# Output products moved among mixer C's last tasks, and four weight units split on GpSimd

## The chip, the cores and the metric

The kernel runs on one core of a Trainium2 chip. The metric is the device time of one execution in microseconds, as the median of several runs. The core has a matrix engine (TensorE), a vector engine (VectorE, DVE in the rows), an activation engine (ScalarE, ACT), a general engine (GpSimd, POOL) and a queue that issues transfers (SyncE, SP). They run side by side and meet only at semaphores. TensorE writes to PSUM, eight banks of 128x512 f32; the rest lies in SBUF.

## The reference

Two layers over 512 tokens of width 1024. Each is one input projection that feeds three token mixers, an output projection, a layer norm, a squared-ReLU MLP and another layer norm:

```
proj = x @ w_in[l]                        # 2578 columns, split into q, k, v, ... of the three mixers
o_a = diff_attention(...)                 # A: 6 heads, softmax(q1 k1) - lam * softmax(q2 k2), times v
o_b = pool_mixer(...)                     # B: causal means over windows 2/4/8/16, 4 groups
o_c = nsa_attention(...)                  # C: 6 heads, compressed + selected + window branch, gated
mix = concat(o_a, o_b, o_c) @ w_out[l]    # 1024 -> 1024
x = layer_norm(ALPHA * x + mix)
hid = square(relu(x @ w_up[l]))           # 4096
x = layer_norm(ALPHA * x + hid @ w_down[l])
```

At this length the selected branch of C takes every block and the window covers the sequence, so both are causal softmax attentions with their own keys and values.

## The kernel before

**Products in three parts.** Weights and activations are split into a high part (rounded to fp32r) and a low part (the rest). `products` makes one 128x512 output tile of one k chunk with three fp32r matmuls, low activation by high weight, high by high, high by low (L682 to L684 where the output has tokens in its partitions). A weight chunk has four *units*, each two k chunks of 128 rows; a unit is 128x1024 in SBUF. SyncE loads it into `raw`, ScalarE's `split_to` makes `w_hi` from it (L1012, counted by `s_hi_ready`), and GpSimd's `split` subtracts to give `w_lo` (L548, `s_lo_ready`). Some units are subtracted on VectorE instead (`low_unit`, L1259). All three buffers are rings of four units: SyncE loads unit u when the low part of u−4 is made, `w_hi` and `w_lo` of u are written when TensorE has used u−4 (`s_unit_used`). Units 28 to 31 (`U_OUT` on) hold the first half (512 columns) of the output weights, 32 to 35 the second.

**Tasks.** Mixers A and C are worked as 33 tasks a layer: 0 to 17 are A, 18 to 32 are C (`TASKS_A` = 18, three pairs of heads with `PAIR_C` = 5 tasks each). A task t has these steps:

- TensorE `scores(t)`: the causal mask and the products of queries and keys of two heads, into banks 2*(t%2) and the one behind (L728/L733 masks, L764/L775 products);
- VectorE `negative_max(t)`: the negated row maxima, read from PSUM (L1399/L1403);
- ScalarE `exps(t)`: the exponentials with their row sums (L1140), counted by `s_exped`;
- VectorE `weights(t)`: reciprocals (L1433), factors with the gates (L1451, in A L1439), and two or four multiplications of the probabilities in SBUF (L1458), counted by `s_probs`;
- TensorE `turn_p(t)`: eight 128x128 transposes into banks 5 and 6 (L787); in A only odd tasks have this and the next two;
- ScalarE `copy_p(t)`: their copy to SBUF (L1149);
- TensorE `values(t)`: the product with the values (L824, in A L809; L818 opens a pair of C).

TensorE's order in iteration t of C is `scores(t+2)`, `turn_p(t)`, `values(t-1)`, then a side step where `SIDE` names one. ScalarE's is `exps(t)`, in four iterations a weight split (`OUT_SPLIT`), `copy_p(t-1)`, then `mt_hi` of the pool mixer (L1194, t = 23 and 24) or of a pair of C (`oc_high`, L1153). VectorE's is `negative_max(t+1)`, `weights(t)`, a side step, in four iterations the low part of a unit, then low parts of `mt`. These orders are written out by hand, and each engine works its list in order.

**Around the change.** GpSimd's last work in the mixers of a layer is the product at L604 for the compressed branch of C; the next is the low part of unit 32. Behind the tasks, TensorE multiplies the mixed heads `mt_hi`, `mt_lo` by the output weights: k chunks 0 and 1 are the pool mixer, 2 to 4 C, 5 to 7 A, whose normalisation ScalarE and VectorE make last. `mixed(k)` waits for chunk k. In `gemm` the first quarter (unit 28, chunks 0 and 1, four banks 0 to 3, 24 matmuls) stands between the turn and the values of task 32, the other three quarters behind that, then the second half of the output columns in banks 4 to 7.

Of the kernel before, what the change touches and what calls it, by code (L numbers as in the profile page):

```python
# [15 lines left out]
F32 = mybir.dt.float32  # L16
F32R = mybir.dt.float32r
BF16 = mybir.dt.bfloat16
ALU = mybir.AluOpType
# [40 lines left out]
IN_CHUNKS = len(IN_COLS)  # L60
LAST = IN_CHUNKS - 1
U_IN, U_LAST, U_OUT, U_MLP = 0, 4 * LAST, 4 * IN_CHUNKS, 4 * IN_CHUNKS + 8
UNITS = U_MLP + 4 * N_MLP
# [13 lines left out]
           12: (13, 14), 13: (15,)}  # L77
LAST_COPIED = {2: 0, 6: 1, 10: 2, 14: 3}
V_BANK = (7, 4)
OUT_SPLIT = (19, 25, 27, 28)  # L80
SIDE = {2: (("compress", 0, 5), ("turn", 9, 6)), 4: (("turn", 10, 5), ("turn", 11, 6)), 6: (("cmp_scores", 0, 5), ("cmp_scores", 1, 6)),
        10: (("square_sums", 0, 5),), 14: (("turn", 13, 5), ("turn", 14, 6)), 15: (("cmp_turn", 0, LAST_BANK),),
        16: (("box", 0, 5), ("box", 1, 6)), 17: (("cmp_turn", 1, LAST_BANK),), 18: (("square_sums", 1, LAST_BANK),),
# [82 lines left out]
def turns(t):  # L166

    return t >= TASKS_A or t % 2 == 1


def turn_number(t):
    return t // 2 if t < TASKS_A else TASKS_A // 2 + t - TASKS_A
# [30 lines left out]
def build(nc, x, w_in, lam_q1, lam_k1, lam_q2, lam_k2, subln_g, w_pool, pool_scale, cmp_pe_k, cmp_pe_v,  # L203
          w_cmp_k, w_cmp_v, w_out, ln1_g, ln1_b, w_up, w_down, ln2_g, ln2_b, consts, out):
    ctx = ExitStack()
    with ctx:
# [109 lines left out]
        def nth(name, layer, n):  # L316

            return layer * PER_LAYER[name] + n
# [214 lines left out]
        def _(pool):  # L533
# [43 lines left out]
            for layer in range(DEPTH):  # L577
                split(layer, 4, U_LAST - 2)
                pool.wait_ge(s_const_in, 32)

                pool.wait_ge(s_turned_act, nth("turned_act", layer, 2))
                pool.wait_ge(s_par_ready, nth("par_ready", layer, 1))
                pool.wait_ge(s_value_weights, nth("value_weights", layer, 16))
                link(rows_to_compress(1))
                split(layer, U_LAST - 2, U_LAST)
                link(rows_to_compress(0))
                nc.gpsimd.memset(ktmp[:, 0:1], 0.0).then_inc(s_cmp_rows, 1)
                split(layer, U_LAST, U_OUT)

                def rope_k(tt):  # L590
                    pool.wait_ge(s_in_copied, nth("in_copied", layer, TT * (LAST - 1) + tt + 1))
                    rotate(nc.gpsimd.tensor_tensor, link, tt, ((T_KSL, 4, 64, R_CCK, R_SCK),)).then_inc(s_roped_k, 1)
                    pool.wait_ge(s_roped_k, nth("roped_k", layer, tt + 1))

                def over24(a):
                    return cst[:, a, :].rearrange("p (i s) -> p i s", i=TT).unsqueeze(3).to_broadcast([P, TT, 6, 32])

                pool.wait_ge(s_cmp_rows, nth("cmp_rows", layer, 1))
                for tt in range(TT):
                    rope_k(tt)  # L600
                pool.wait_ge(s_cmp_max, nth("cmp_max", layer, 1))
                nc.gpsimd.tensor_tensor(cmp_s, cmp_s, over24(0), ALU.subtract).then_inc(s_cmp_shifted, 1)
                pool.wait_ge(s_cmp_factor, nth("cmp_factor", layer, 1))
                nc.gpsimd.tensor_tensor(cmp_s, cmp_s, over24(3), ALU.mult).then_inc(s_cmp_probs, 1)  # L604

                split(layer, U_OUT + 4, U_MLP + 2)
                rstd_of(layer, 0)
                split(layer, U_MLP + 4, UNITS)
                if layer < DEPTH - 1:
                    split(layer + 1, 0, 2)  # L610
                rstd_of(layer, 1)
# [3 lines left out]
        def _(pe):  # L615
# [303 lines left out]
            for layer in range(DEPTH):  # L919
# [36 lines left out]
                def mixed(k):  # L956
# [5 lines left out]
                    elif k >= M_C:  # L962
                        pe.wait_ge(s_oc_mixed, nth("oc_mixed", layer, k - M_C + 1))

                for t in range(TASKS):
                    if t < 2 * BOTH - 2 and t % 2:
                        scores_of_both(layer, t + 1)
                    for n in LAST_AT.get(t, ()):
                        last_chunk(layer, n)
                    if 2 * BOTH - 2 <= t < TASKS - 2:  # L970
                        scores(layer, t + 2)
                    if turns(t):
                        turn_p(layer, t)
                    if t >= 1 and turns(t - 1):
                        values(layer, t - 1)
                    if t in SIDE:
                        side(layer, t)
                pe.wait_ge(s_exped, nth("exped", layer, TASKS))
                gemm(layer, IN_CHUNKS, 0, mt_hi, mt_lo, mixed, (0,))
                values(layer, TASKS - 1)  # L980
                gemm(layer, IN_CHUNKS, 0, mt_hi, mt_lo, mixed, (1, 2, 3))
                gemm(layer, IN_CHUNKS + 1, 4, mt_hi, mt_lo, mixed, by_bank=2, ahead=lambda: turn_half(layer, 1, 0))

                for k in range(N_MLP):
# [16 lines left out]
        def _(act):  # L1001
# [75 lines left out]
            for layer in range(DEPTH):  # L1077
# [88 lines left out]
                for t in range(TASKS):  # L1166
                    if t >= 2:
                        exps(t)
                    if t in OUT_SPLIT:
                        split_to(layer, U_OUT + OUT_SPLIT.index(t) + 1)  # L1170
                    if t == 10:
                        act.wait_ge(s_cmp_shifted, nth("cmp_shifted", layer, 1))
                        by_tile = cmp_s.rearrange("p i s n -> p i (s n)")
                        A(by_tile, by_tile, ACT.Exp).then_inc(s_cmp_exp, 1)
                    if t and turns(t - 1):
                        copy_p(t - 1)
                    if t in LAST_COPIED:
                        b = LAST_COPIED[t]
                        if b < 3:
                            act.wait_ge(s_last_done, nth("last_done", layer, b + 1))  # L1180
                        else:
                            act.wait_ge(s_unit_used, nth("unit_used", layer, U_OUT))
                        copy_in(layer, LAST, b)
                    if t - 1 in SIDE:
                        side(t - 1)
                    if t in (PAIR + 1, 2 * PAIR + 1, 3 * PAIR + 1):
                        pair = t // PAIR - 1
                        act.wait_ge(s_pv, nth("pv", layer, turn_number(PAIR * (pair + 1))))
                        A(oa[:, pair], ps[:, V_BANK[0], :], ACT.Copy)
                        A(rms[:, pair], ps[:, V_BANK[0], :], ACT.Square).then_inc(s_oa_squared, 1)  # L1190
                    if t in (23, 24):

                        act.wait_ge(s_side_emptied, nth("side_emptied", layer, SIDE_END[t - 2]))
                        A(mt_hi[:, M_POOL + t - 23], pooled[:, t - 23], ACT.Copy).then_inc(s_pool_hi, 1)  # L1194
                    if t in (TASKS_A + PAIR_C + 1, TASKS_A + 2 * PAIR_C + 1):
                        oc_high((t - TASKS_A) // PAIR_C - 1)
                copy_p(TASKS - 1)
                act.wait_ge(s_side_emptied, nth("side_emptied", layer, SIDES))
                flat = rms[:].rearrange("p a q -> p (a q)")
                A(flat, flat, ACT.Ln).then_inc(s_chain_act, 1)  # L1200
# [32 lines left out]
        def _(dve):  # L1233
# [103 lines left out]
            for layer in range(DEPTH):  # L1337
# [129 lines left out]
                for t in range(TASKS):  # L1467
# [28 lines left out]
                    if t == 13:  # L1496
# [2 lines left out]
                        fv = cst[:, 2, :].rearrange("p (i j g) -> p i j g", i=TT, j=HG)  # L1499
                        ov = cst[:, 3, :].rearrange("p (i j g) -> p i j g", i=TT, j=HG)  # L1500
                        V.tensor_tensor(ov, fv, gv, ALU.mult).then_inc(s_cmp_factor, 1)
                    if t - 1 in OUT_SPLIT:
                        low_unit(layer, U_OUT + OUT_SPLIT.index(t - 1))
                    if t in (24, 25):
                        c = t - 24
                        dve.wait_ge(s_pool_hi, nth("pool_hi", layer, c + 1))
# [99 lines left out]
```

## Time and profile before

| | |
|---|---|
| median of 3 runs | 1258.08 us (1258.02 to 1258.6) |
| profiled execution | 1258.8 us, span 1257.0 us |
| mean granted clock of TensorE | 0.998 of full |
| TensorE busy | 1236.8 us (98%) |
| VectorE busy | 725.4 us (58%) |
| ScalarE busy | 477.7 us (38%) |
| GpSimd busy | 489.1 us (39%) |
| matmuls of the output product (L682 to L684 with mt) | 3 x 384 |
| loads of the output weights | 8 of 512 KB, 12 of 256 KB |

Columns of the views below: a timeline row has start (us from the start of the span), duration (us), engine, line and operation, output<-inputs, shape, how many in a row were merged, and in brackets the idle time before with what ended it. In a chain row the duration is the piece of the chain. Matmuls are pipelined and their recorded durations overlap, so the time of a series is read from the starts. L12 is line 12 of the kernel.

### The profile page before, as it was taken

To read this page: it belongs to the slowest core of one execution; us is meant where nothing else is said; L and a number is where in the kernel's file an instruction comes from. 1 tells how busy PE (TensorE), PEld (TensorE's weight loads), DVE (VectorE), ACT (ScalarE), POOL (GpSimd) and SP (SyncE) were. 2 spreads that over 40 slices of the span, in tenths; PEclk is the share of its full clock that TensorE was granted. 3 is DMA by queue.
4 is the path that set the end of the run, shared out by engine and by line. 5 is a ranking of instruction groups with operands and counts; after the bars stand their busy time and mean duration, and the time that the engine had idled before them with its cause. 6 is when DMAs were issued, how large, how long until landed. Compare 5 with 4: busy or idle time off the path is not lost.

```text
span 1257.0 us, 18648 instructions
## 1 busy us (share of the span) xinstructions
PE 1236.8 (98%) x7514; PEld 1027.3 (82%) x7514; DVE 725.4 (58%) x1120; ACT 477.7 (38%) x946; POOL 489.1 (39%) x277
## 2 busy tenths in 40 slices
PE   7999999999999999999999999999999999999997
PEld 7998666789888888888899976668988888888885
DVE  4396778369672262360397867783796623605406
ACT  5226688523232221222143366784333312222210
POOL 1468000134444444444345760003264444444442
PEclk9999999999999999999999999999999999999999
DMA  7433001123523332333224320012233332223211
GB/s 254 127 81 102 2 18 35 68 84 102 163 94 101 101 99 88 99 101 96 63 59 127 94 69 1 19 52 101 68 130 105 101 101 87 99 101 101 92 60 67
DMA packets 77973, 110.28 MB, mean 88 GB/s; under 512 B 17664, under 2 KB 38336, under 8 KB 77760
## 3 DMA queue, kind: packets, MB, share of 16 engines
q1 hardware_dynamic: 76304, 104.31, 26.6%
q10 hardware_dynamic: 1584, 4.78, 1.1%
q8 instruction: 60, 0.98, 0.3%
q14 instruction: 25, 0.20, 0.1%
HBM read 106.98 MB, written 2.10 MB: 87 GB/s over the span
## 4 chain that ended last, share of the span: by engine, by line
PE 92%; DVE 4%; ACT 1%; issue 1%; POOL 1%; DMA 0%; DVEq 0%; ACTq 0%; POOLq 0%
PE ps L682 16%; PE ps L684 16%; PE ps L683 16%; PE ps L678 9%; PE ps L679 9%; PE ps L680 9%; PE ps L787 3%; PE ps L775 3%; PE ps L824 2%; PE ps L637 1%; PE ps L809 1%; DVE negmax L1403 1%; ACT probs_a L1140 1%; PE ps L900 1%; PE ps L862 1%
## 5 line engine op out<-in xcount | busy, mean ns | idle before, releaser
L548 POOL TENSOR_TENSOR w_lo<-raw,w_hi 128x1024 fp32r<-128x1024 f32 (+3 forms) x182 | 421.1, 2319 | 647.6 <-ACT w_hi L1012 647.2
L1012 ACT ACTIVATE w_hi<-raw 128x1024 fp32r<-128x1024 f32 (+3 forms) x200 | 199.0, 996 | 598.8 <-PE ps L684 364.5
L678 PE MATMUL ps<-xt_hi,w_lo 128*128 128x512 f32 (+1 forms) x576 | 210.7, 366 | 0.0
L679 PE MATMUL ps<-xt_hi,w_hi 128*128 128x512 f32 (+1 forms) x576 | 210.5, 365 | 0.0
L680 PE MATMUL ps<-xt_lo,w_hi 128*128 128x512 f32 (+1 forms) x576 | 210.5, 365 | 0.0
L682 PE MATMUL ps<-w_hi,xt_lo 128*128 128x384 f32 (+3 forms) x448 | 152.6, 341 | 0.7 <-DVE xt_lo L1248 0.3
L682 PE MATMUL ps<-w_hi,mt_lo 128*128 128x512 f32 x384 | 150.1, 391 | 0.0
L683 PE MATMUL ps<-w_hi,mt_hi 128*128 128x512 f32 x384 | 149.4, 389 | 0.0
L684 PE MATMUL ps<-w_lo,mt_hi 128*128 128x512 f32 x384 | 149.4, 389 | 0.0
L683 PE MATMUL ps<-w_hi,xt_hi 128*128 128x384 f32 (+3 forms) x448 | 148.1, 331 | 0.0
L684 PE MATMUL ps<-w_lo,xt_hi 128*128 128x384 f32 (+3 forms) x448 | 148.0, 330 | 0.0
L680 PEld LDWEIGHTS ps<-xt_lo,w_hi 128*128 128x128 f32 x576 | 108.5, 188 | 17.6
L678 PEld LDWEIGHTS ps<-xt_hi,w_lo 128*128 128x128 f32 x576 | 108.5, 188 | 17.4
L679 PEld LDWEIGHTS ps<-xt_hi,w_hi 128*128 128x128 f32 x576 | 108.5, 188 | 17.4
L1530 DVE TENSOR_TENSOR xres<-xres,ps 128x512 f32<-128x512 f32 x48 | 32.9, 685 | 132.9 <-PE ps L684 132.1
L682 PE MATMUL ps<-w_hi,he_lo 128*128 128x512 f32 x256 | 99.6, 389 | 0.0
L683 PE MATMUL ps<-w_hi,he_hi 128*128 128x512 f32 x256 | 99.6, 389 | 0.0
L684 PE MATMUL ps<-w_lo,he_hi 128*128 128x512 f32 x256 | 99.6, 389 | 0.0
L1557 DVE TENSOR_TENSOR mt_lo<-tmp,mt_hi 128x512 fp32r<-128x512 f32 x32 | 71.3, 2229 | 47.9 <-ACT mt_hi L1229 47.9
L1565 DVE TENSOR_SCALAR tmp<-ps 128x512 f32<-128x512 f32 x64 | 44.1, 690 | 89.6 <-PE ps L680 88.5
L682 PEld LDWEIGHTS ps<-w_hi,xt_lo 128*128 128x128 f32 x448 | 85.1, 190 | 11.0 <-issue 6.3
L1557 DVE TENSOR_TENSOR he_lo<-tmp,he_hi 128x512 fp32r<-128x512 f32 x32 | 65.6, 2049 | 38.8 <-ACT he_hi L1229 38.8
(175 smaller groups left out, 1868.1 us busy)
## 6 DMA issues: line engine op xcount, KB each, us to landing
raw<-in_w_up SPq DMA_DIRECT2D x64, 512.0 KB, 3.4
raw<-in_w_down SPq DMA_DIRECT2D x64, 512.0 KB, 3.8
raw<-in_w_in SPq DMA_DIRECT2D x32, 384.0 KB, 3.3
raw<-in_w_in SPq DMA_DIRECT2D x16, 256.0 KB, 2.8
raw<-in_w_in SPq DMA_DIRECT2D x32, 128.0 KB, 2.5
raw<-in_w_out SPq DMA_DIRECT2D x8, 512.0 KB, 3.2
raw<-in_w_out SPq DMA_DIRECT2D x12, 256.0 KB, 3.7
rows<-in_ln_g ACTq DMA_DIRECT2D x4, 512.0 KB, 4.3
```

The costliest lines, as they stand in the source:

```text
L548: nc.gpsimd.tensor_tensor(unit_of(w_lo, u), unit_of(raw, u), unit_of(w_hi, u).bitcast(F32), ALU.subtract).then_inc(s_lo_ready, 1)
L678: mm(o, wl[:, c], a_hi[:, k, cols], start=first, stop=False)
L679: mm(o, wh[:, c], a_hi[:, k, cols], start=False, stop=False)
L680: return mm(o, wh[:, c], a_lo[:, k, cols], start=False, stop=end)
L682: mm(o, a_lo[:, k, c], wh, start=first, stop=False)
L683: mm(o, a_hi[:, k, c], wh, start=False, stop=False)
L684: return mm(o, a_hi[:, k, c], wl, start=False, stop=end)
L775: last = mm(o[:, at_:at_ + n], queries, keys, start=False, stop=True, skip_group_check=True)
L787: last = nc.tensor.transpose(ps[:, P_BANK + hh, j * P:(j + 1) * P], probs_of(t)[:, hh, j * P:(j + 1) * P], ident)
L1012: A(unit_of(w_hi, u), unit_of(raw, u), ACT.Copy).then_inc(s_hi_ready, 1)
L1557: V.tensor_tensor(lo[:, f], tmp[:, f % 2], hi[:, f].bitcast(F32), ALU.subtract) \
L1565: link(V.tensor_scalar(tmp[:, f % 2], ps[:, bank + b, :], 0.0, None, ALU.max))
```

## The change

- `OUT_SPLIT` and its uses on ScalarE and VectorE go. GpSimd, behind its product at L604, waits for the turn of task 18 and then makes, for units 28 to 31 in order, `w_hi` with a copy and, when that has landed, `w_lo` with a subtraction. ScalarE waits once, behind its copy of task 32, for `w_hi` of unit 31.
- From task 19 on TensorE works `values(t-1)` ahead of `turn_p(t)`.
- `first_of_out`: in iteration 31 chunks 0 and 1 into banks 2 and 3, and in iteration 32 into banks 0 and 1, 12 matmuls each, ahead of the values and the turn of the iteration. `second_of_out`: chunk 2 into all four banks ahead of `values(32)`, chunk 3 behind it. The third and fourth quarter follow as before.

```diff
--- before.py
+++ after.py
@@ -77,7 +77,6 @@
            12: (13, 14), 13: (15,)}
 LAST_COPIED = {2: 0, 6: 1, 10: 2, 14: 3}
 V_BANK = (7, 4)
-OUT_SPLIT = (19, 25, 27, 28)
 SIDE = {2: (("compress", 0, 5), ("turn", 9, 6)), 4: (("turn", 10, 5), ("turn", 11, 6)), 6: (("cmp_scores", 0, 5), ("cmp_scores", 1, 6)),
         10: (("square_sums", 0, 5),), 14: (("turn", 13, 5), ("turn", 14, 6)), 15: (("cmp_turn", 0, LAST_BANK),),
         16: (("box", 0, 5), ("box", 1, 6)), 17: (("cmp_turn", 1, LAST_BANK),), 18: (("square_sums", 1, LAST_BANK),),
@@ -603,6 +602,16 @@
                 pool.wait_ge(s_cmp_factor, nth("cmp_factor", layer, 1))
                 nc.gpsimd.tensor_tensor(cmp_s, cmp_s, over24(3), ALU.mult).then_inc(s_cmp_probs, 1)
 
+                pool.wait_ge(s_p_turned, nth("p_turned", layer, turn_number(TASKS_A) + 1))
+                for u in range(U_OUT, U_OUT + 4):
+                    g = layer * UNITS + u
+                    pool.wait_ge(s_raw[u % RING], raw_landed(layer, u))
+                    pool.wait_ge(s_unit_used, g - RING + 1)
+                    nc.gpsimd.tensor_copy(unit_of(w_hi, u), unit_of(raw, u)).then_inc(s_hi_ready, 1)
+                    pool.wait_ge(s_hi_ready, nth("hi_ready", layer, u + 1))
+                    nc.gpsimd.tensor_tensor(unit_of(w_lo, u), unit_of(raw, u), unit_of(w_hi, u).bitcast(F32),
+                                            ALU.subtract).then_inc(s_lo_ready, 1)
+
                 split(layer, U_OUT + 4, U_MLP + 2)
                 rstd_of(layer, 0)
                 split(layer, U_MLP + 4, UNITS)
@@ -962,6 +971,28 @@
                     elif k >= M_C:
                         pe.wait_ge(s_oc_mixed, nth("oc_mixed", layer, k - M_C + 1))
 
+                def first_of_out(layer, t):
+
+                    pe.wait_ge(s_exped, nth("exped", layer, t + 1))
+                    pe.wait_ge(s_lo_ready, nth("lo_ready", layer, U_OUT + 1))
+                    pe.wait_ge(s_hi_ready, nth("hi_ready", layer, U_OUT + 1))
+                    for k in range(2):
+                        mixed(k)
+                        for b in (2 * (t % 2), 2 * (t % 2) + 1):
+                            last = products(IN_CHUNKS, k, b, 0, mt_hi, mt_lo)
+                    if t == TASKS - 1:
+                        last.then_inc(s_unit_used, 1)
+
+                def second_of_out(layer, k):
+
+                    pe.wait_ge(s_lo_ready, nth("lo_ready", layer, U_OUT + 2))
+                    pe.wait_ge(s_hi_ready, nth("hi_ready", layer, U_OUT + 2))
+                    mixed(k)
+                    for b in range(4):
+                        last = products(IN_CHUNKS, k, b, 0, mt_hi, mt_lo)
+                    if k == 3:
+                        last.then_inc(s_unit_used, 1)
+
                 for t in range(TASKS):
                     if t < 2 * BOTH - 2 and t % 2:
                         scores_of_both(layer, t + 1)
@@ -969,16 +1000,22 @@
                         last_chunk(layer, n)
                     if 2 * BOTH - 2 <= t < TASKS - 2:
                         scores(layer, t + 2)
-                    if turns(t):
+                    if t >= TASKS - 2:
+                        first_of_out(layer, t)
+                    if t > TASKS_A:
+                        values(layer, t - 1)
                         turn_p(layer, t)
-                    if t >= 1 and turns(t - 1):
-                        values(layer, t - 1)
+                    else:
+                        if turns(t):
+                            turn_p(layer, t)
+                        if t >= 1 and turns(t - 1):
+                            values(layer, t - 1)
                     if t in SIDE:
                         side(layer, t)
-                pe.wait_ge(s_exped, nth("exped", layer, TASKS))
-                gemm(layer, IN_CHUNKS, 0, mt_hi, mt_lo, mixed, (0,))
+                second_of_out(layer, 2)
                 values(layer, TASKS - 1)
-                gemm(layer, IN_CHUNKS, 0, mt_hi, mt_lo, mixed, (1, 2, 3))
+                second_of_out(layer, 3)
+                gemm(layer, IN_CHUNKS, 0, mt_hi, mt_lo, mixed, (2, 3))
                 gemm(layer, IN_CHUNKS + 1, 4, mt_hi, mt_lo, mixed, by_bank=2, ahead=lambda: turn_half(layer, 1, 0))
 
                 for k in range(N_MLP):
@@ -1166,8 +1203,6 @@
                 for t in range(TASKS):
                     if t >= 2:
                         exps(t)
-                    if t in OUT_SPLIT:
-                        split_to(layer, U_OUT + OUT_SPLIT.index(t) + 1)
                     if t == 10:
                         act.wait_ge(s_cmp_shifted, nth("cmp_shifted", layer, 1))
                         by_tile = cmp_s.rearrange("p i s n -> p i (s n)")
@@ -1195,6 +1230,8 @@
                     if t in (TASKS_A + PAIR_C + 1, TASKS_A + 2 * PAIR_C + 1):
                         oc_high((t - TASKS_A) // PAIR_C - 1)
                 copy_p(TASKS - 1)
+                act.wait_ge(s_hi_ready, nth("hi_ready", layer, U_OUT + 4))
+                done[0] = U_OUT + 4
                 act.wait_ge(s_side_emptied, nth("side_emptied", layer, SIDES))
                 flat = rms[:].rearrange("p a q -> p (a q)")
                 A(flat, flat, ACT.Ln).then_inc(s_chain_act, 1)
@@ -1499,8 +1536,6 @@
                         fv = cst[:, 2, :].rearrange("p (i j g) -> p i j g", i=TT, j=HG)
                         ov = cst[:, 3, :].rearrange("p (i j g) -> p i j g", i=TT, j=HG)
                         V.tensor_tensor(ov, fv, gv, ALU.mult).then_inc(s_cmp_factor, 1)
-                    if t - 1 in OUT_SPLIT:
-                        low_unit(layer, U_OUT + OUT_SPLIT.index(t - 1))
                     if t in (24, 25):
                         c = t - 24
                         dve.wait_ge(s_pool_hi, nth("pool_hi", layer, c + 1))
```

## Rows read from the trace of the kernel before

**Rows 1.** The page: busy us, share of the span, instructions of TensorE.
```profile
PE 1236.8 (98%) x7514; PEld 1027.3 (82%) x7514; DVE 725.4 (58%) x1120; ACT 477.7 (38%) x946; POOL 489.1 (39%) x277
```

**Rows 2.** The chain that ended last, 190 to 262 us: start, us, what.
```profile
223.25 1.04 PE ps L787 x8
...
227.10 0.89 DVE probs L1458 x2
...
228.06 1.07 PE ps L787 x8
...
230.15 0.43 PE ps L682
230.58 0.23 PE ps L683
```

**Rows 3.** The same chain in layer 1, 810 to 890 us.
```profile
847.96 1.07 PE ps L787 x8
```

**Rows 4.** Timeline of TensorE, 222 to 240 us.
```profile
224.20 1.09 PE L824 MATMUL ps<-p_t,proj_v 128*64 128x128 f32 x16
225.76 1.09 PE L787 MATMUL ps<-kc,probs 128*128 128x128 f32 x8 [0.47 <-DVE probs L1458]
...
228.06 1.07 PE L787 MATMUL ps<-kc,probs 128*128 128x128 f32 x8 [0.18 <-DVE probs L1458]
```

**Rows 5.** Timeline of all engines, 168 to 197 us: tasks 18 to 20.
```profile
176.14 1.09 PE L787 MATMUL ps<-kc,probs 128*128 128x128 f32 x8
...
177.60 1.06 ACT L1012 ACTIVATE w_hi<-raw 128x1024 fp32r<-128x1024 f32 x1
...
177.96 0.17 DVE L1451 TENSOR_TENSOR facs<-recs,gates 128x4 f32<-128x4 f32 x1
178.16 1.14 DVE L1458 TENSOR_SCALAR probs<-probs,facs 128x384 f32<-128x384 f32 x4
...
178.54 1.02 ACT L1149 ACTIVATE p_t<-ps 128x1024 f32<-128x1024 f32 x1
...
180.48 1.09 PE L787 MATMUL ps<-kc,probs 128*128 128x128 f32 x8
...
183.84 1.22 DVE L1259 TENSOR_TENSOR w_lo<-raw,w_hi 128x1024 fp32r<-128x1024 f32 x1
...
184.77 1.09 PE L787 MATMUL ps<-kc,probs 128*128 128x128 f32 x8
```

**Rows 6.** GpSimd's groups by form: count, busy us, mean ns, idle before.
```profile
L548 POOL TENSOR_TENSOR w_lo<-raw,w_hi 128x1024 fp32r<-128x1024 f32 x140 | 343.1, 2455 | 552.5 <-ACT w_hi L1012 552.2
...
L562 POOL MEMSET cmp_wv<- 128x32 f32 x2 | 0.3, 159 | 0.0
L576 POOL MEMSET w_blk<- 128x256 f32 x1 | 0.3, 312 | 0.3 <-POOLq L1596 0.3
```

**Rows 7.** VectorE's and GpSimd's timelines at 124 us; VectorE's group in mixer C.
```profile
124.36 1.89 DVE L1458 TENSOR_SCALAR probs_a<-probs_a,recs 128x512 f32<-128x512 f32 x2
...
124.37 0.73 POOL L436 TENSOR_TENSOR proj_k<-proj_k,kc 128x256 f32<-128x256 f32 x1
125.18 0.79 POOL L440 TENSOR_TENSOR proj_k<-proj_k,ktmp 128x256 f32<-128x256 f32 x1
...
L1458 DVE TENSOR_SCALAR probs<-probs,facs 128x512 f32<-128x512 f32 x24 | 10.6, 483 | 0.4
```

**Rows 8.** The two timelines at 142 us, and VectorE's maxima at 121 us.
```profile
141.92 1.33 DVE L1439 TENSOR_TENSOR facs<-recs,lams 128x2 f32<-128x2 f32 x1
...
141.76 1.48 POOL L602 TENSOR_TENSOR proj_b<-proj_b,cst 128x768 f32<-128x768 f32 x1 [15.79 <-DVE cst L1482]
...
121.42 2.36 DVE L1403 TENSOR_REDUCE negmax<-ps 128x2 f32<-128x1024 f32 x2
```

**Rows 9.** The two timelines at 298 us.
```profile
298.22 3.42 DVE L1266 TENSOR_TENSOR xres<-xres,rows 128x1024 f32<-128x1024 f32 x1
...
297.31 9.93 POOL L548 TENSOR_TENSOR w_lo<-raw,w_hi 128x1024 fp32r<-128x1024 f32 x3
```

## The prediction

> **What bounds the kernel now.** I read the page's busy shares first: TensorE is busy for 1236.8 us of a span of 1257.0 [rows 1]. Then the chain of waits over the end of mixer C [rows 2]: the scores of task 32, the turn of task 30 and so on follow each other without a gap, about 3.3 us of TensorE work per task, until the scores run out. Only there does the chain leave TensorE, for the exponentials, the factors and the multiplications of task 32, and it comes back at 228.06. Layer 1 repeats it, with that turn at 847.96 [rows 3]. TensorE's timeline shows what can be won there: it sits idle 0.47 us before the turn of task 31 and 0.18 us before that of task 32 [rows 4]. By the starts and the chain's 1.02 us a block it is (225.76 − 225.22) + (228.06 − 227.80) = 0.8 us a layer, 1.6 us in all. Within mixer C no gap is left to fill, so any gain of this change is bounded by 1.6 us, 0.13%. The question is what it puts beside VectorE, whose multiplications end half a microsecond or so before TensorE turns their result.
>
> **The change part by part.**
>
> *Output product among the last tasks.* The 24 matmuls of the first quarter, which stood behind task 32, are cut into two blocks of 12 ahead of tasks 31 and 32 (banks 2 and 3, then 0 and 1, as the exponentials free them), and the second quarter into two blocks of 12. The number of matmuls is the same; each costs 0.23 us. The first block, 12 × 0.23 = 2.7 us, covers the whole chain from the exponentials of task 32 to its multiplications, so the 0.8 us go. What is paid: the first fp32r matmul behind a turn or a values step takes 0.43 us for 0.23 [rows 2]. There are two such entries before and four after, so 2 × 0.2 = 0.4 us come back. Net 0.8 − 0.4 = 0.4 us less a layer. What is late next is the third third of mixer C's output: it comes from values of task 32, which now has one block less of 2.7 us behind it before its own product; by the same steps it still is ready more than 1 us ahead, so I cost it at nothing.
>
> *Values ahead of turns, tasks 19 to 32.* No instruction more. TensorE works scores (about 1.27 us), values, turn. The values step of task t−1 needs ScalarE's copy of 1.02 us behind its turn [rows 5], some 0.1 us with the two hand-overs: 1.15 us against 1.27 us, so a margin of 0.1 us, once ScalarE is free. Where ScalarE has a further 0.6 us piece in a task (tasks 23, 24, 29) it can run over. I cost it at 0, bound it at 3 × 0.5 = 1.5 us a layer. Below nothing it cannot go, as TensorE has no gap there.
>
> *Both parts of four units on GpSimd.* Removed: four ScalarE copies of 1.06 us and four VectorE subtractions of 1.22 us a layer [rows 5]; neither engine sets the end there, so they give back nothing but ScalarE's room for the step above. Added: on GpSimd, right behind the turn of task 18, four times a copy and a subtraction. The subtraction has its row: 2.455 us in the mean of 140, some of them disturbed by VectorE [rows 6]; I take 2.4 us. No GpSimd copy stands in the trace. From below, the memset rows give 0.159 us + 992 × (0.312 − 0.159)/224 = 0.84 us for 1024 columns; from above, the subtraction with its two inputs, 2.4 us. I take 1.1 us, near the memset, which like the copy has one stream to write and no second input. The Trainium skill, GPSIMD Engine Reference, section 4.1, calls one-input work "roughly line-rate"; at its 1.2 GHz that is an estimate of 0.85 us, and the sum would be 2 us lower; no row here shows it.
>
> GpSimd was idle there, so its 4 × (1.1 + 2.4) = 14 us a layer seem free. They are not, by the rows of mixer A. There VectorE's multiplication of the probabilities (128x512, SBUF to SBUF), which in mixer C takes 0.48 us, came as a pair of 1.89 us while two short GpSimd instructions ran, the first from 124.37 for 0.73, the second from 125.18 for 0.79 [rows 7]: each of the two waited until one of GpSimd's had ended. A factor product, 0.17 us alone [rows 5], took 1.33 us, to the end of GpSimd's 1.48 us [rows 8]. Long ones alternate: from 298 us VectorE's products of 128x1024 with two SBUF inputs, a size and form that takes 1.22 us alone [rows 5], took 3.42 us while GpSimd's three took 9.93 us [rows 9]. The maxima, read from PSUM, are not held: 1.18 us each beside GpSimd [rows 8]. So of a mixer C task the factor product and each of the two or four multiplications can wait out one whole GpSimd instruction, the maxima and the reciprocals none.
>
> The Trainium skill, SBUF — State Buffer, section "Who interferes with whom", states the same lock, held for a whole instruction by whichever issues first, and speaks against this placement. It leaves open whether consecutive multiplications keep the lock; if they do, the sum is the one-wait rival's below, and rows 7 speak against that.
>
> Laid out for layer 0 from the rows of tasks 19 and 20 [rows 5]:
> - 177.3 to 178.4 first copy. The factor product of task 19, due at 177.96, runs at 178.4; subtraction to 181.1; first multiplication; copy to 182.5; second; subtraction to 185.3; third; copy to 186.6; fourth, done 186.9 where it was 179.3. The turn of task 19 starts at 186.9, not 180.48.
> - The third subtraction, to 189.1, runs partly beside the maxima. Factor product of task 20; copy to 190.3; one multiplication; last subtraction to 192.9; the other three, done 193.9. The turn of task 20 starts at 193.9, not 184.77: 9.1 us late. Of that 1.0 us is the values step that now stands ahead of it, so 8.1 us are lost.
> - After that GpSimd is through and TensorE is full again up to the end.
>
> Sum: 8.1 − 0.4 = 7.7 us a layer, 15.4 us for two. The profiled execution of before took 1258.8 us (span 1257.0), 0.7 us over the median of the three runs, 1258.1: 1274.2 on its own base, 1273.5 us for the median. Each 0.1 us of the copy is worth 4 × 0.1 a layer, 0.8 us in all: 1271.4 us at 0.84 us, 1283.9 us at 2.4 us.
>
> GpSimd's queue: what stands behind the four units waits for ScalarE's parts of the second half, needed some 40 us later, so nothing behind it is late. The next loads on SP hang on the finished low parts and come earlier or at about the same time.
>
> **The rivals.**
> 1. *No lock for these forms, or it hides* (not slower). GpSimd's 14 us lie beside everything, and only the 0.4 us a layer are left: 1257.3 us. For it: the copy is a form that the trace does not hold. Against: rows 7 are the very multiplications of mixer C. It decides only if TensorE's start of the turns of tasks 19 and 20 stays within about 1 us of scores and values.
> 2. *One wait a task.* VectorE keeps the lock for its multiplications once it has it; a task loses at most one subtraction, most of it in the 1.5 us that it has to spare in the new order: about 1 us a layer, 1260 us. Against: the pair of 1.89 us.
> 3. *Two or more multiplications pass between GpSimd's instructions*, since a 128-column one is short: the turn of task 19 comes at about 183, that of task 20 at 189.5, and the rest falls into task 21: about 5 us a layer less 0.4, 1267.5 us.
> 4. *ScalarE's copy becomes the wait* of the values step. Alone it would be 1.5 − 0.4 = 1.1 us a layer, 1260.3 us, from the point where ScalarE's work in a task is above 3.3 us. It can add up to 3 us to the forecast.
>
> **How the numbers follow.** A measurement of this kernel tells about 0.2%, 2.5 us, from no change. Forecast with the copy between 0.84 and 2.4 us: 0.60. Rival 3: 0.15. Rivals 2 and 4, about 1260 to 1262: 0.10, half of it within 2.5 us. Rival 1: 0.10, within. Faster by over 2.5 us would need more than all of TensorE's idle time here; 0.05 for what I do not see. That makes slower 0.80, same 0.15, faster 0.05. The range goes from 1259.5 us (leaving out rival 1 and faster, 0.15) to 1281 us (leaving out a copy above 2 us, 0.05).
>
> **What would show it.** GpSimd: eight instructions a layer from 177 us, stretched to about 193 us. VectorE: multiplications of 1 to 2.5 us in tasks 19 and 20, and 0.3 to 0.5 us ones after. TensorE: idle before two turns, 6 to 9 us together. At the tail, no idle before the turns of tasks 31 and 32, and four entries of 0.43 us. I am wrong if the multiplications keep their 0.28 to 0.48 us beside GpSimd, or if the copy is far from 1.1 us.

## The result, and the profile after

The changed kernel takes 1266.97 us (median of 4 runs, 1266.53 to 1267.21) against 1258.05 us: ratio 1.0073, 95% interval 1.0061 to 1.0085, so 8.9 us slower. The forecast was 1273.5 us, in a range of 1259.5 to 1281: sign and mechanism as forecast, the loss a little over half of the forecast 15.4 us. The profiled execution took 1266.99 us, its span is 1265.1 us.

TensorE's timeline of tasks 19 and 20 stands against [rows 5]. Columns are as ahead of the prediction; line numbers are those of the changed kernel (L796 is the turn, L784 scores, L833 values, L1495 the multiplications, L1488 the factor product, L610 and L612 GpSimd's copy and subtraction).

```profile
175.26 1.10 PE L796 MATMUL ps<-kc,probs 128*128 128x128 f32 x8
...
184.54 1.55 PE L796 MATMUL ps<-kc,probs 128*128 128x128 f32 x8 [2.84 <-DVE probs L1495]
...
186.25 2.08 PE L784 MATMUL ps<-ks,qc 64*128 64x512 f32 x4
188.26 1.16 PE L833 MATMUL ps<-p_t,proj_v 128*64 128x128 f32 x16
190.97 1.09 PE L796 MATMUL ps<-kc,probs 128*128 128x128 f32 x8 [1.55 <-DVE probs L1495]
```

Both turns wait for VectorE's multiplications, 2.84 and 1.55 us. From the turn of task 18 on, the turn of task 19 comes 9.28 us later (before: 180.48 − 176.14 = 4.34), that of task 20 15.71 us later (before: 8.63). The second is 7.08 us late, of which 1.02 us is the values step that now stands ahead of it: 6.06 us. What held VectorE, from its timeline and GpSimd's over the same stretch:

```profile
177.07 0.41 DVE L1488 TENSOR_TENSOR facs<-recs,gates 128x4 f32<-128x4 f32 x1
177.51 6.97 DVE L1495 TENSOR_SCALAR probs<-probs,facs 128x384 f32<-128x384 f32 x4
...
186.33 0.53 DVE L1488 TENSOR_TENSOR facs<-recs,gates 128x4 f32<-128x4 f32 x1
186.89 4.02 DVE L1495 TENSOR_SCALAR probs<-probs,facs 128x256 f32<-128x256 f32 x4
...
192.35 0.88 DVE L1495 TENSOR_SCALAR probs<-probs,facs 128x512 f32<-128x512 f32 x2
```

```profile
176.42 1.04 POOL L610 CAST w_hi<-raw 128x1024 fp32r<-128x1024 f32 x1 [15.15 <-PE ps L796]
177.54 2.35 POOL L612 TENSOR_TENSOR w_lo<-raw,w_hi 128x1024 fp32r<-128x1024 f32 x1
179.83 1.17 POOL L610 CAST w_hi<-raw 128x1024 fp32r<-128x1024 f32 x1
181.08 2.34 POOL L612 TENSOR_TENSOR w_lo<-raw,w_hi 128x1024 fp32r<-128x1024 f32 x1
183.36 1.04 POOL L610 CAST w_hi<-raw 128x1024 fp32r<-128x1024 f32 x1
184.48 2.36 POOL L612 TENSOR_TENSOR w_lo<-raw,w_hi 128x1024 fp32r<-128x1024 f32 x1
186.78 1.04 POOL L610 CAST w_hi<-raw 128x1024 fp32r<-128x1024 f32 x1
187.90 2.34 POOL L612 TENSOR_TENSOR w_lo<-raw,w_hi 128x1024 fp32r<-128x1024 f32 x1
```

The four multiplications of task 19 take 6.97 us where they took 1.14. They end at 184.48, just behind GpSimd's third copy (184.40): one multiplication passes behind each of subtraction, copy, subtraction, copy. The factor products end with a copy (177.48 behind 177.46) and with a subtraction (186.86 behind 186.84). In task 20 the multiplications end 0.7 us behind the last subtraction, and in task 21 they are back at 0.88 us. This agrees with the Trainium skill, SBUF — State Buffer, section "Who interferes with whom": the pair of ports is held for a whole instruction. So VectorE and GpSimd meet here without any semaphore between them, against what the text ahead of the prediction says of the engines. GpSimd's own instructions hardly stretch: 13.8 us from first to last, 1.04 to 1.17 and 2.34 to 2.36 us each.

TensorE's granted clock fell behind its gap, which the forecast did not have. Each row below has the stretch and its length, the busy time of TensorE, its weight loads, VectorE, ScalarE and GpSimd (in brackets the instructions), then the granted clock as a share of full, the busy share of the DMA engines and GB/s:

```profile
182.00:184.00 2.00, 0.00 (x0) 0.00 (x0) 2.00 (x2) 0.00 (x0) 2.00 (x2) 1.00 0.30 117
185.00:188.00 3.00, 3.00 (x18) 1.30 (x16) 2.93 (x6) 1.88 (x4) 2.92 (x3) 0.50 0.56 170
188.00:190.00 2.00, 1.42 (x18) 0.92 (x16) 2.00 (x1) 0.48 (x2) 2.00 (x1) 0.89 0.71 224
```

At half clock (1.2 GHz) the scores are recorded with 2.08 us instead of 1.13; the turn before them, during which the clock falls, takes 1.48 us to the next start instead of 1.02. Here that costs nothing: TensorE is idle for 1.55 us again afterwards.

Layer 1 repeats layer 0: waits of 2.83 and 1.55 us, and the turn of task 20 comes 15.70 us behind that of task 18.

The tail, where the output product went, against [rows 2, 4], and for the entry the two rows of the kernel before that these do not hold:

```profile
228.76 1.09 PE L796 MATMUL ps<-kc,probs 128*128 128x128 f32 x8
229.61 0.47 PE L691 MATMUL ps<-w_hi,mt_lo 128*128 128x512 f32 x1
229.92 0.40 PE L692 MATMUL ps<-w_hi,mt_hi 128*128 128x512 f32 x1
...
242.13 1.09 PE L833 MATMUL ps<-p_t,proj_v 128*64 128x128 f32 x16
243.16 0.50 PE L691 MATMUL ps<-w_hi,mt_lo 128*128 128x512 f32 x1
243.50 0.40 PE L692 MATMUL ps<-w_hi,mt_hi 128*128 128x512 f32 x1
```

```profile
230.08 0.50 PE L682 MATMUL ps<-w_hi,mt_lo 128*128 128x512 f32 x1
230.42 0.40 PE L683 MATMUL ps<-w_hi,mt_hi 128*128 128x512 f32 x1
```

No gap stands there any more. A turn and the first fp32r matmul behind it take 229.92 − 228.76 = 1.16 us, a values step and the first one behind it 243.50 − 242.13 = 1.37 us. The usual step of 1.02 us and the usual matmul of 0.23 us would be 1.25 us. On the way out of a block its last matmul takes 0.32 us for 0.23 (232.23 to 232.55). So with its exit a block behind a turn costs nothing, one behind values 0.2 us.

### The profile page after: what moved, and what is told of

It reads as the page before. It is cut to its first block, busy times and chain, and to the rows that moved or that the text cites. A ratio compares the mean times of both kernels' runs of the same rounds, so it can differ in the third digit from the quotient of the medians.

```text
span 1265.1 us, 18648 instructions
## 1 busy us (share of the span) xinstructions
PE 1237.8 (98%) x7514; PEld 1027.2 (81%) x7514; DVE 735.0 (58%) x1112; ACT 469.9 (37%) x938; POOL 516.0 (41%) x293
## 4 chain that ended last, share of the span: by engine, by line
PE 89%; DVE 6%; ACT 2%; issue 1%; POOL 1%; DMA 0%; DVEq 0%; ACTq 0%; POOLq 0%
PE ps L691 16%; PE ps L692 16%; PE ps L693 16%; PE ps L687 9%; PE ps L688 9%; PE ps L689 9%; PE ps L796 3%; PE ps L784 2%; PE ps L833 2%; DVE probs L1495 2%; PE ps L646 1%; ACT probs_a L1177 1%; DVE negmax L1440 1%; PE ps L818 1%; ACT probs L1177 1%
## 5 line engine op out<-in xcount | busy, mean ns | idle before, releaser
L1049 ACT ACTIVATE w_hi<-raw 128x1024 fp32r<-128x1024 f32 (+3 forms) x192 | 190.2, 993 | 593.4 <-PE ps L693 361.2
```

The lines of the kernel that those rows point to most:

```text
L1049: A(unit_of(w_hi, u), unit_of(raw, u), ACT.Copy).then_inc(s_hi_ready, 1)
```

## The experiments

Theory L: GpSimd's eight instructions hold the port of VectorE's multiplications, and their time in a row is what the turns of tasks 19 and 20 wait for; the new order by itself gains a little. Rival O: the new order costs, as values wait for ScalarE's copies. Rival T: GpSimd beside VectorE costs wherever it lies. The kernel before took 1257.70 us beside the first four runs and 1257.81 us beside the last four.

**The order alone.** The changed kernel without GpSimd's part; the four units are split as before.

```diff
 (GpSimd)
-                pool.wait_ge(s_p_turned, nth("p_turned", layer, turn_number(TASKS_A) + 1))
-                for u in range(U_OUT, U_OUT + 4):
-                    ...
 (ScalarE, VectorE)
+                    if t in OUT_SPLIT:
+                        split_to(layer, U_OUT + OUT_SPLIT.index(t) + 1)
-                act.wait_ge(s_hi_ready, nth("hi_ready", layer, U_OUT + 4))
+                    if t - 1 in OUT_SPLIT:
+                        low_unit(layer, U_OUT + OUT_SPLIT.index(t - 1))
```

> The changed kernel with its new TensorE order (values ahead of turns, first quarters of the output product among tasks 31 and 32), but with the four units split on ScalarE and VectorE as before. Theory L (GpSimd's eight instructions hold the port of VectorE's multiplications, and that alone makes the changed kernel slower): the order gives back 1.1 to 1.6 us a layer, by the idle 0.8 us of the tail and the entries behind a turn, which cost less than those behind a values step: 1255 to 1256 us against 1258.05. Rival O (the order costs, because values wait for ScalarE's copies): 1260 us or more, and TensorE idle in front of the values steps.

Measured: 1256.56 us, ratio 0.9988 (0.9979 to 0.9997). Rival O falls as the cause of the loss. The gain of 1.1 us is half of what was expected. TensorE's timeline in layer 0 shows why:

```profile
178.32 1.13 PE L775 MATMUL ps<-ks,qc 64*128 64x512 f32 x4
179.57 1.07 PE L818 MATMUL ps<-cmp_pt,vcmp 32*64 32x512 f32 x4
...
204.39 1.09 PE L824 MATMUL ps<-p_t,proj_v 128*64 128x128 f32 x16 [0.28 <-ACT p_t L1177]
...
214.66 1.09 PE L824 MATMUL ps<-p_t,proj_v 128*64 128x128 f32 x16 [0.16 <-ACT p_t L1177]
```

Two values steps wait for ScalarE's copy. A third wait is not marked: L818 starts 1.25 us behind the scores, where it is 1.06 us in the changed kernel. In the code it needs a square that ScalarE makes at L1218, which ends at 179.42, as it stands behind the weight split of task 19. By the starts of the turns these three cost 0.8 us a layer in both layers: from the turn of task 18 to that of task 30 it is 48.22 us, in the paced kernel below 47.45.

**GpSimd's part alone,** in the kernel before.

```diff
 (GpSimd)
+                pool.wait_ge(s_p_turned, nth("p_turned", layer, turn_number(TASKS_A) + 1))
+                for u in range(U_OUT, U_OUT + 4):
+                    ... (copy to w_hi, subtraction to w_lo, as in the change)
 (ScalarE, VectorE: the uses of OUT_SPLIT go)
```

> The kernel before with GpSimd making both parts of the four units and nothing else changed. Theory L: the turn of task 20 comes some 7.1 us late in each layer, as in the changed kernel, and here no values step is already done ahead of it, so the whole 7 us are lost: 1258 + 14 = 1272 us. Rival O: GpSimd's work costs nothing by itself, 1258 us.

Measured: 1274.57 us, ratio 1.0133 (1.0119 to 1.0147): 16.9 us slower, 8 us more than the whole change and 2.9 us more than expected. TensorE's timeline:

```profile
175.25 1.09 PE L796 MATMUL ps<-kc,probs 128*128 128x128 f32 x8
...
184.52 1.97 PE L796 MATMUL ps<-kc,probs 128*128 128x128 f32 x8 [4.87 <-DVE probs L1467]
186.42 1.97 PE L827 MATMUL ps<-cmp_pt,vcmp 32*64 32x512 f32 x4
188.32 1.98 PE L833 MATMUL ps<-p_t,proj_v 128*64 128x128 f32 x16
...
192.07 1.09 PE L796 MATMUL ps<-kc,probs 128*128 128x128 f32 x8
```

and the stretches of it, columns as above:

```profile
180.00:182.00 2.00, 0.00 (x0) 0.00 (x0) 2.00 (x3) 0.50 (x3) 1.92 (x2) 0.84 0.44 136
182.00:184.00 2.00, 0.00 (x0) 0.00 (x0) 2.00 (x2) 0.00 (x0) 2.00 (x2) 0.50 0.33 126
...
186.00:188.00 2.00, 2.00 (x7) 0.38 (x5) 1.93 (x5) 1.47 (x2) 1.92 (x3) 0.50 0.52 119
188.00:190.00 2.00, 2.00 (x18) 1.57 (x16) 2.00 (x1) 0.89 (x4) 2.00 (x1) 0.50 0.80 222
```

The turn of task 19 comes at the same moment as in the changed kernel (9.27 us behind that of task 18). But the 2 us of L827 and values of task 18, which the changed order works in the gap, here stand behind it, and TensorE works them at half clock: 4.87 us idle, then 1.97, 1.97 and 1.98 us for steps of about 1.1 us. The turn of task 20 starts with no wait of its own, 16.82 us behind that of task 18 where before it was 8.63: 8.2 us lost, 16.4 in two layers. So in this kernel the fallen clock is on the path, and in the changed one it is not. VectorE's multiplications of task 20 end at 190.90 here too, so the clock costs 1.1 us a layer, and the other 1.0 us by which this kernel is worse at task 20 is the values step that the changed order has already worked. These 2.1 us a layer are half of the 8 us between the two kernels; most of the rest is what the new order gains elsewhere (below).

**The quarters alone,** turns ahead of values.

```diff
 (the definitions of first_of_out and second_of_out come in as in the change)
+                    if t >= TASKS - 2:
+                        first_of_out(layer, t)
...
-                gemm(layer, IN_CHUNKS, 0, mt_hi, mt_lo, mixed, (0,))
+                second_of_out(layer, 2)
                 values(layer, TASKS - 1)
-                gemm(layer, IN_CHUNKS, 0, mt_hi, mt_lo, mixed, (1, 2, 3))
+                second_of_out(layer, 3)
+                gemm(layer, IN_CHUNKS, 0, mt_hi, mt_lo, mixed, (2, 3))
```

> The kernel before with only the output product's first two quarters moved among tasks 31 and 32; turns stay ahead of values, units split as before. Here the blocks stand behind values steps, where an entry costs 0.2 us. By the prediction's own sum: 0.8 us of idle time filled, two entries more, 0.4 us less a layer, 1257.3 us. If the entry costs less than that, up to 0.9 us a layer, 1256.3 us. Rival (the tail behind task 32 becomes late, since the third part of C is ready only behind the moved values step): over 1258.5 us, with TensorE idle before the third quarter.

Measured: 1256.93 us, ratio 0.9994 (0.9985 to 1.0003). The median is 0.8 us lower, the size of the prediction's sum for this part; the interval holds no change too. The trace has the size more sharply: from the turn of task 18 to the end of the second quarter it is 65.72 us where the kernel before takes 66.20. The rival's 1258.5 us is out.

**The values alone** ahead of the turns.

```diff
-                    if turns(t):
+                    if t > TASKS_A:
+                        values(layer, t - 1)
                         turn_p(layer, t)
-                    if t >= 1 and turns(t - 1):
-                        values(layer, t - 1)
```

> The kernel before with only the values ahead of the turns from task 19 on. ScalarE still has its four weight copies of 1.06 us in tasks 19, 25, 27 and 28. If these make the values step wait: about 1.3 us more a layer, 1260.6 us, and TensorE's idle time stands before the values steps of those tasks. If the copies are in time: 0.2 us less for each of the side steps of tasks 20 to 22, 0.6 us a layer, 1256.8 us, less what the tail loses as there is one turn behind the last values step.

Measured: 1261.08 us, ratio 1.0025 (1.0016 to 1.0034). The size is as expected, the place is not. TensorE's timeline at the tail:

```profile
225.25 1.09 PE L824 MATMUL ps<-p_t,proj_v 128*64 128x128 f32 x16 [1.11 <-ACT p_t L1153]
...
228.48 1.09 PE L824 MATMUL ps<-p_t,proj_v 128*64 128x128 f32 x16 [1.11 <-ACT p_t L1153]
```

Two of the four gaps, 2.2 us of 2.65 us in layer 0, stand where there are no scores left between a turn and the values that need its copy. Only 0.27 and 0.16 us, and the 0.2 us ahead of L818 as above, are owed to crowded ScalarE tasks. So the two parts of the new order belong together: the output blocks stand just in these two places.

**Each copy twice,** in the changed kernel.

```diff
+                    link(nc.gpsimd.tensor_copy(unit_of(w_hi, u), unit_of(raw, u)))
                     nc.gpsimd.tensor_copy(unit_of(w_hi, u), unit_of(raw, u)).then_inc(s_hi_ready, 1)
```

> The changed kernel with each of GpSimd's four copies issued twice, so four instructions of 1.04 us more a layer. Theory L (GpSimd's back-to-back time, 13.8 us from the turn of task 18 on, is what the turn of task 20 waits for): nearly all of it arrives. Two of the additional instructions are passed by the maxima of a further task, so between 3 and 4.2 us a layer: 1273 to 1275.3 us against 1266.97. Rival T (what costs is the number of tasks whose weights fall beside GpSimd, or the clock that falls in the gap, not GpSimd's time): under 1269 us.

Measured: 1272.05 us (ratio 1.0111, 1.0097 to 1.0124), 5.1 us above the changed kernel: 2.5 us a layer for 4.2 us of GpSimd time. The expectation of 3 us or more is missed. Rival T's bound of 1269 us is passed, but the traces show that this run does not decide against it, since most of the 5.1 us is clock. VectorE's timeline:

```profile
177.38 4.87 DVE L1496 TENSOR_SCALAR probs<-probs,facs 128x384 f32<-128x384 f32 x4
...
185.64 5.63 DVE L1496 TENSOR_SCALAR probs<-probs,facs 128x256 f32<-128x256 f32 x4
...
192.51 2.16 DVE L1489 TENSOR_TENSOR facs<-recs,gates 128x2 f32<-128x2 f32 x1
```

A multiplication waits for whichever GpSimd instruction its turn falls behind. Task 19 now met a copy, a subtraction and a copy, and its last multiplication slipped by in the hand-over between two linked copies; so it was done over 2 us earlier (4.87 for 6.97 us). Part of the rest moved into task 20, whose turn comes 0.5 us later than in the changed kernel (16.20 us behind that of task 18 for 15.71). The 2.16 us of the factor product of task 21 cost next to nothing: its multiplications end at 195.59, when TensorE at full clock would just come to that turn (191.33 + 4.21 = 195.54). TensorE does not come to it then:

```profile
191.33 1.97 PE L797 MATMUL ps<-kc,probs 128*128 128x128 f32 x8 [5.67 <-DVE probs L1496]
193.09 1.91 PE L872 MATMUL ps<-rms,kc 128*128 128x512 f32 x2
...
197.25 1.09 PE L797 MATMUL ps<-kc,probs 128*128 128x128 f32 x8
```

```profile
190.00:192.00 2.00, 0.67 (x3) 0.67 (x4) 2.00 (x3) 0.00 (x0) 1.94 (x3) 0.50 0.20 65
192.00:194.00 2.00, 2.00 (x9) 1.42 (x7) 1.97 (x3) 0.67 (x1) 1.92 (x2) 0.50 0.69 198
```

The waits before tasks 19 and 20 have become 0.74 and 5.67 us, and behind the long one TensorE works at half clock. The turn of task 21 comes 5.92 us behind that of task 20, in layer 1 6.57 us, where the changed kernel has 4.21 in both. So of the 5.1 us some 4 are the fallen clock, and some 1.2 are VectorE's waits.

**GpSimd paced.** Each of the eight instructions waits for the end of the weights of one task.

```diff
+PACE = ((19, 20), (21, 22), (23, 26), (27, 28))
-                pool.wait_ge(s_p_turned, nth("p_turned", layer, turn_number(TASKS_A) + 1))
                 for u in range(U_OUT, U_OUT + 4):
                     ...
+                    pool.wait_ge(s_probs, nth("probs", layer, PACE[u - U_OUT][0] + 1))
                     nc.gpsimd.tensor_copy(...)
                     pool.wait_ge(s_hi_ready, nth("hi_ready", layer, u + 1))
+                    pool.wait_ge(s_probs, nth("probs", layer, PACE[u - U_OUT][1] + 1))
                     nc.gpsimd.tensor_tensor(...)
```

> The changed kernel with GpSimd's eight instructions paced: each waits until VectorE has finished the weights of a certain task (19, 20, 21, 22, 23, 26, 27, 28). Behind the weights of a task VectorE uses no shared port for about 2.4 us (maxima from PSUM, reciprocals, waiting), so the copies of 1.04 us and the subtractions of 2.35 us lie there. Theory L: the loss of 8.9 us goes, and with ScalarE's and VectorE's splits gone the order gains what it gained in the order-only kernel or up to 0.5 us a layer more: 1255.5 to 1256.6 us. Rival T (GpSimd beside VectorE costs wherever it lies): over 1262 us.

Measured: 1254.97 us, ratio 0.9977 (0.9968 to 0.9986), 12.0 us below the changed kernel with the same instructions on the same engines, and 2.8 us below the kernel before. GpSimd's timeline, then VectorE's behind the first subtraction:

```profile
183.00 2.35 POOL L614 TENSOR_TENSOR w_lo<-raw,w_hi 128x1024 fp32r<-128x1024 f32 x1 [2.93 <-DVE probs L1497]
```

```profile
184.46 1.23 DVE L1442 TENSOR_REDUCE negmax<-ps 128x2 f32<-128x1024 f32 x1 [1.60 <-PE ps L786]
185.61 0.17 DVE L1472 RECIPROCAL recs<-sums 128x2 f32<-128x2 f32 x1
185.81 0.16 DVE L1490 TENSOR_TENSOR facs<-recs,gates 128x2 f32<-128x2 f32 x1
186.00 0.88 DVE L1497 TENSOR_SCALAR probs<-probs,facs 128x512 f32<-128x512 f32 x2
```

The subtraction ends at 185.35, beside the maxima, and the factor product and the multiplications keep their 0.16 and 0.88 us. Rival T falls here: place decides, not presence. Two later subtractions do reach a factor product (1.20 us at 209.39 and 0.53 us at 216.47, for 0.16), but VectorE is done in time all the same: in layer 0 TensorE has no gap left from task 18 to the output product.

**GpSimd short.** The changed kernel with copies and subtractions on 16 of the 512 columns of each chunk; the other columns of the four units are left out.

```diff
-                    nc.gpsimd.tensor_copy(unit_of(w_hi, u), unit_of(raw, u)).then_inc(s_hi_ready, 1)
+                    nc.gpsimd.tensor_copy(unit_of(w_hi, u)[:, :, 0:16], unit_of(raw, u)[:, :, 0:16]).then_inc(s_hi_ready, 1)
```

> The changed kernel with GpSimd's copies and subtractions of the four units made on 16 of the 512 columns of each chunk, so that eight short instructions stand where eight long ones stood; the other columns keep what the ring held (this part of the work is left out). It prices GpSimd's time as a whole. Theory L: 1255.5 to 1256.6 us, the order's gain alone. Rival T: over 1260 us.

Measured: 1254.40 us, ratio 0.9972 (0.9962 to 0.9983). This is the price of GpSimd's time as a whole: 1266.97 − 1254.40 = 12.6 us, 6.3 a layer, beside the 6.06 us that the turn of task 20 showed in layer 0. Everything else in the change gains 3.4 us. The paced kernel is 0.6 us above it, but not in mixer C: from the turn of task 18 to the first matmul of the output product the two traces have 48.30 and 48.29 us. So paced, GpSimd's work costs TensorE nothing there.

**Paced, turns ahead of values.** The paced kernel with the old order of turns and values.

```diff
-                    if t > TASKS_A:
-                        values(layer, t - 1)
-                        turn_p(layer, t)
-                    else:
                     ...
```

> As the paced kernel, but with the turns ahead of the values as in the kernel before, the output product's quarters moved. In the kernel with GpSimd's work alone this order lost 16.9 us, since TensorE had no values step to work in the gap and its clock fell to half. Theory L: paced, there is no gap, and the order makes little difference: 1256.5 to 1257.5 us, near the quarter-only kernel (1256.93). Rival: the turns-first order has less room on VectorE's path, and a subtraction of 2.35 us reaches into it: over 1259 us.

Measured: 1256.65 us, ratio 0.9991 (0.9982 to 1.0). So even the order that lost 16.9 us with GpSimd's work in a row loses nothing when it is paced. (This kernel has the moved quarters too, which the one that lost 16.9 us had not.) It is 1.7 us above the paced kernel with values first.

## Why the prediction was right, and where it was mis-sized

*The lock and the alternation* were the step that carried the sign, and both held: the rows of mixer A told the right thing of a placement in mixer C. Rivals 1 and 2 needed multiplications that keep their time or wait once; they took 6.97 and 4.02 us. Rival 3 lies at 1267.5 us, half a microsecond from the measured time, and yet is not what happened: its two multiplications per gap appear nowhere in task 19.

*The laid-out schedule* was too long. Its instructions had the right price: the copy 1.04 us for the assumed 1.1, the subtraction 2.35 for 2.4. The Trainium skill, GPSIMD Engine Reference, section 4.1, "roughly line-rate", gave an estimate of 0.85 us; the row stands 0.2 us above it. The error was in the hand-overs. I let each passing factor product or multiplication push GpSimd's next instruction back by 0.2 to 0.35 us. In the trace GpSimd's instructions follow at 0.1 us or less, and the row of eight ended at 190.24 where mine, set to the same turn of task 18 (0.88 us earlier), would have ended at 192.0: 1.5 of these 1.8 us are hand-overs, 0.3 the instructions. So the turn of task 20 came 7.08 us late for 9.1, and GpSimd's part cost 6.1 to 6.3 us a layer for 8.1: 12.6 us for 16.2. The sign that I named, 6 to 9 us of idle time before the two turns, was missed too: it is 4.39 us, as the turn and the scores between the two gaps were worked at half clock and filled some of it.

*The order* was sized at 0.4 us a layer of gain, and the whole change but GpSimd's time gains 1.7 (3.4 us in both). In the trace of the kernel with GpSimd short, 1.5 us of it stand in mixer C: from the turn of task 18 to the end of the second quarter it takes 64.69 us for 66.20. For the quarters by themselves the sum fitted (0.48 us a layer by the traces). What was missing is what the values step ahead of the turn does for its neighbours. I took 0.2 us for every entry, from a row of 0.43 us that stood behind a values step. Behind a turn it is nothing, and the new order puts three of its four entries there, so the tail gains 0.9 us. The same holds for the side steps of tasks 20 to 22: behind a turn instead of a values step each is about 0.2 us shorter, and from the turn of task 20 to that of task 30 the changed kernel takes 37.79 us where it took 38.41. ScalarE's removed pieces I had as room for the values step, and that was right: the changed kernel has no wait for ScalarE there, and the order-only kernel, which keeps them, loses 0.8 us a layer by it.

*Values ahead of turns* I costed as a small risk. It was a cover too: it gave TensorE 2 us of work in the gap that GpSimd opened and kept its clock off the path. With GpSimd's part and the old order the loss was 16.9 us, near the forecast 15.4, and the fallen clock that is part of it was not in the forecast; that the two figures are near is chance. *Rival 4*, ScalarE's copy as the wait, is real only where output blocks or scores are missing (1.11 us twice a layer) and, with ScalarE's splits kept, in the order-only kernel; the changed kernel has none of it.

*What stays open.* The span grew by 8.1 us, while mixer C and its tail cost 4.55 us in each layer (70.75 us for 66.20 from the turn of task 18 to the end of the second quarter in layer 0; layer 1 has the same turns). Mixer C of layer 0 began 0.88 us earlier in the profiled execution of the changed kernel (175.26 for 176.14), in a stretch that the change does not touch. The starts in the other kernels lie between 174.84 and 175.71 us, so I take it for a difference between executions; no run shows what it comes from. Differences of some 0.5 us between medians, as the 0.6 us between the paced and the short kernel, are of this kind and carry no reading.

## What to carry to other kernels

GpSimd is not free room beside VectorE. Before work is moved there, list VectorE's SBUF-to-SBUF multiplications and its instructions with two SBUF inputs in that stretch: here each could be held for a whole GpSimd instruction, and each instruction of the row but the last let one of them pass behind it. If the work must go there, make each instruction wait for the end of VectorE's last port-using step of a period, and check that the stretch up to the next one is as long as the instruction, or that VectorE has the time to spare where it is not; here that turned 8.9 us lost into 2.8 us gained. Where more such work makes a kernel slower, look at the granted clock behind the longest gap before you put it all down to the lock. Two changes of order can be a loss and a small gain alone (3.4 us lost and 0.8 us gained here) and belong together, so price them in the combination, by what stands in each gap.

## What the runs showed of the hardware that was not expected

- GpSimd's instructions were not slowed by VectorE's short ones: 1.04 to 1.17 us and 2.34 to 2.36 us in a row of eight, while VectorE's multiplications went from some 0.4 us to up to 2.59 us (the first one of task 19, at 177.51). Here the engine with the short instructions pays for the alternation.
- TensorE's granted clock was 0.50 (1.2 GHz) from 185 to 188 us behind an idle time of 2.84 us. In the kernel with GpSimd's part alone it was 0.50 from 182 to 190 us, in and behind an idle time of 4.87 us; in the one with the copies doubled from 190 to 194 us, in and behind one of 5.67 us. A gap can cost more than its length: 1.1 us more a layer in the first of these two kernels, 1.6 and 2.3 us in the second, and nothing in the changed kernel, where TensorE waited again.
- The first fp32r matmul behind a series of transposes of 128 columns cost nothing extra (1.16 us for both); behind the values series it was 0.2 us later (1.37 us).
